# Hybrid encoder trunk on one core: where the second half of V's work sits at the turn from dots to dense products

## What is computed

```
def peer(xn, wq, k1, k2, u, v):
    ...                                     # idx: (token, 128) experts, gate: their softmax
    def block(args):                        # 128 tokens
        x_blk, i_blk, g_blk = args
        act = gelu(einsum('td,ted->te', x_blk, u[i_blk]))
        return einsum('te,ted->td', g_blk * act, v[i_blk])
    return lax.map(block, (xb, ib, gb))
```

## Time and profile before

| | |
|---|---|
| median of 3 runs | 3210.08 us (3208.91 to 3210.76) |
| the profiled execution: its time, its span | 3210.99 us, 3209.2 us |
| busy share of the span | DVE 77%, PE 68%, POOL 51%, ACT 27% |
| DMA over the span | 1096.32 MB, mean 342 GB/s |
| one gather of u: POOL's issue | 1.78 us, 496 of them |
| one dot on DVE | 2.29 us, 512 of them |
| one V addition on DVE | 1.28 us, 456 of them |
| TensorE's granted clock, mean | 0.841 of full speed |

### The profile page before, as it was taken

The page is one execution under the profiler, slowest core; times in us unless marked ns, Lnnn a source line. Parts: engine busy times, 40 slices in busy tenths (PEclk is TensorE's granted clock), DMA queues, the critical chain, the costliest instruction groups (busy, mean ns, idle before and its releaser), DMA issues.

```text
span 3209.2 us, 23725 instructions
## 1 busy us (share of the span) xinstructions
PE 2180.4 (68%) x7652; PEld 1394.4 (43%) x7652; DVE 2474.9 (77%) x3537; ACT 856.6 (27%) x1749; POOL 1621.2 (51%) x1051
## 2 busy tenths in 40 slices
PE   7999984440233348999979999444014344799999
PEld 6887773330121234444437878333012223444444
DVE  4454588999999986655575767999999998766666
ACT  4344410000555672000003442000036556400000
POOL 1000045666788834655560103555677884466665
PEclk9999996775567689999999999676556666999999
DMA  6554589999999957999994437999999997699999
GB/s 231 184 184 144 183 339 417 418 406 370 417 416 420 420 234 305 414 413 411 412 368 139 163 107 305 406 422 403 395 390 416 421 419 298 243 414 413 414 413 379
DMA packets 231210, 1096.32 MB, mean 342 GB/s; under 512 B 23208, under 2 KB 23984, under 8 KB 144176
## 3 DMA queue, kind: packets, MB, share of 16 engines
q0 software_dynamic: 147456, 805.37, 62.0%
q1 hardware_dynamic: 80256, 282.22, 23.2%
q10 hardware_dynamic: 3376, 7.23, 0.7%
HBM read 1092.63 MB, written 2.11 MB: 341 GB/s over the span
## 4 chain that ended last, share of the span: by engine, by line
DVE 32%; DMA 29%; PE 19%; issue 9%; POOL 8%; ACT 4%; ACTq 0%; DVEq 0%; SPq 0%; POOLq 0%
DVE ring_sb L1996 20%; PE bank L1118 15%; DMA actT_sb<-in_peer_vg_dram,idx_all 13%; DMA ring_sb<-in_peer_vg_dram,idx_all 8%; DMA ring_sb<-in_peer_u_dram,idx_all 6%; POOL ring_sb L639 5%; DVE x_sb L1970 3%; POOL actT_sb L656 2%; ACT ring_sb L904 1%; POOL ring_sb L656 1%; DVE shared L1709 1%; DVE shared L1705 1%; DVE pair_all L1713 1%; PE bank L1328 1%; POOL ring_sb L615 0%
## 5 line engine op out<-in xcount | busy, mean ns | idle before, releaser
L639 POOL DMA_INDIRECT ring_sb<-in_peer_u_dram,idx_all x496 | 880.8, 1776 | 378.1 <-DVE idx_all L1714 236.1
L1996 DVE CUSTOM_DVE_ANT_0 ring_sb<-ring_sb,actT_sb 128x2048 f32<-128x2048 f32 x256 | 572.5, 2285 | 26.1 <-DMA ring_sb<-in_peer_u_dram,idx_all 25.8
L1996 DVE CUSTOM_DVE_ANT_0 ring_sb<-ring_sb,arena 128x2048 f32<-128x2048 f32 x256 | 574.6, 2285 | 21.2 <-DMA ring_sb<-in_peer_u_dram,idx_all 19.6
L1970 DVE SCALAR_TENSOR_TENSOR x_sb<-actT_sb,gate_rows,x_sb 128x1024 f32<-128x1024 f32 x300 | 384.4, 1284 | 214.4 <-DMA actT_sb<-in_peer_vg_dram,idx_all 212.0
L1118 PE MATMUL bank<-w_parts,actT_hi 128*128 128x512 f32 x1664 | 521.0, 394 | 7.0 <-DVE w_parts L445 4.9
L656 POOL DMA_INDIRECT actT_sb<-in_peer_vg_dram,idx_all x300 | 370.3, 1234 | 296.0 <-DVE x_sb L1970 247.6
L1408 PE MATMUL bank<-ring_sb,arena 128*128 128x512 f32 x1024 | 481.3, 592 | 2.3 <-issue 2.3
L1408 PE MATMUL bank<-ring_sb 128*128 128x512 f32 x1024 | 481.2, 592 | 0.0
L1384 PE MATMUL bank<-gain 128*128 128x128 f32 x768 | 144.5, 351 | 411.8 <-ACT gain L885 386.5
L1165 PE MATMUL bank<-arena 128*128 128x256 f32 x896 | 248.1, 443 | 233.0 <-DVE shared L1996 233.0
L445 DVE TENSOR_TENSOR w_parts<-ring_sb,w_parts 128x2048 fp32r<-128x2048 f32 x100 | 229.3, 2298 | 211.9 <-ACT w_parts L439 211.8
(11 more groups left out here) (214 smaller groups left out, 2193.5 us busy)
## 6 DMA issues: line engine op xcount, KB each, us to landing
ring_sb<-in_peer_vd_dram SPq DMA_DIRECT2D x128, 1024.0 KB, 8.0
ring_sb<-in_mlstm_w_in_dram SPq DMA_DIRECT2D x48, 1024.0 KB, 5.1
arena<-in_peer_wq_dram SPq DMA_DIRECT2D x28, 1024.0 KB, 13.6
ring_sb<-in_attn_w_in_dram SPq DMA_DIRECT2D x20, 1024.0 KB, 5.1
ring_sb<-in_mlstm_w_out_dram SPq DMA_DIRECT2D x16, 1024.0 KB, 5.0
ring_sb<-in_attn_w_out_dram SPq DMA_DIRECT2D x16, 1024.0 KB, 5.0
ring_sb<-in_peer_u_dram,idx_all POOLq DMA_INDIRECT x496, 11.5
actT_sb<-in_peer_vg_dram,idx_all POOLq DMA_INDIRECT x300, 10.2
```

The costliest lines, as they stand in the source:

```text
L639: nc.gpsimd.indirect_dma_start(out=ring[i % NU], out_offset=None, in_=u_tab[l], in_offset=bass.IndirectOffsetOnAxis(ap=rows_at, axis=0),). ...
L1970: v.scalar_tensor_tensor(out=xb[b][:, DENSE:D], in0=g_slot[G_SLOT[j]], scalar=w_all[b][:, p:p + 1], in1=xb[b][:, DENSE:D], op0=ALU.mult, o ...
L1996: v.tensor_tensor_reduce(ring[i % NU], ring[i % NU], rows[b], 1.0, 0.0, ALU.mult, ALU.add, dots[u % 2][:, k:k + 1]).then_inc(dot_done, 1)
```

## The change

The first three loads of the ordered half all wait for the layer's last dot and for the last use of the rows gathered ahead. DVE makes no addition among the groups; all 228 come behind the last one. The gathers take the six places in plain order, so that gather 4 is the first in place 4, and the wait for all groups' products stands ahead of it.

```diff
@@ -334,8 +334,7 @@
         G_ALL = len(G_ORDER)
         G_LAST = [max(j for j in range(G_ALL) if G_ORDER[j][0] == b) for b in range(NB)]
         G_SAME = [max([-1] + [i for i in range(j) if G_ORDER[i][0] == G_ORDER[j][0]]) for j in range(G_ALL)]
-        G_EARLY = 12
-        G_SLOT = [j % 4 if j < G_EARLY else (j - G_EARLY) % NG for j in range(G_ALL)]
+        G_SLOT = [j % NG for j in range(G_ALL)]
         G_USE = [G_SLOT[:j].count(G_SLOT[j]) for j in range(G_ALL)]
         G_BEFORE = [max([-1] + [i for i in range(j) if G_SLOT[i] == G_SLOT[j]]) for j in range(G_ALL)]
 
@@ -526,11 +525,10 @@
             def load_dense(l):
 
                 for p in range(D_PAIRS):
-                    if p < ND - 1:
-                        sp.wait_ge(dot_done, l * LAYER_TILES + LAYER_TILES - NU + 2 + p + 1)
-                    elif p < ND:
+                    if p == 0:
+                        sp.wait_ge(dot_done, (l + 1) * LAYER_TILES)
                         sp.wait_ge(ahead_used, (l + 1) * N_AHEAD)
-                    else:
+                    if p >= ND:
                         sp.wait_ge(vd_used, l * D_PAIRS + p - ND + 1)
                     sp.dma_start(d_slot[p % ND], vd_tab[l][p]).then_inc(vd_landed[p % ND], 16)
                     if l == 0 and p in KEYS_BEHIND:
@@ -649,7 +647,7 @@
                     pool.wait_ge(idx_ready, (l + 1) * UNITS)
                 elif j < 4:
                     pool.wait_ge(ahead_used, (l + 1) * N_AHEAD)
-                if j == G_EARLY + 4:
+                if j == 4:
                     pool.wait_ge(wb_full, (2 * l + 2) * GROUPS)
                 if G_BEFORE[j] >= 0:
                     pool.wait_ge(vg_added, l * G_ALL + G_BEFORE[j] + 1)
@@ -2026,8 +2024,6 @@
                 wait_groups(dve, GR[f"t{l}"] + 1, 1)
                 for g in range(GROUPS):
                     weighted_group(g)
-                    if g % 4 == 3:
-                        add_value()
                 while added[0] < G_ALL:
                     if l == 0 and added[0] in KEYS_SPLIT:
                         lo_weights(dve, 16, [KEYS_SPLIT.index(added[0])])
```

## The result

The changed kernel takes 3217.2 us (median of 14 runs, 3213.43 to 3219.57), the kernel before 3211.16 beside it (3208.86 to 3214.86). The ratio is 1.0018 with a 95% interval of 1.0011 to 1.0026: some 6 us slower, where 4.4 were forecast. The profiled execution has a span of 3215.3 us against 3209.2. In a later series the same kernel had 1.0014 (1.0004 to 1.0023), 4.6 us. So the price is some 5 or 6 us by the medians, and the two intervals leave anything from 1 to 8.

A forecast was written before the change was run, and what follows sets the result against it. DMA bandwidth and PE's dense products bound the dense stage nearly alike. Layer 1: -7.4 + 0 + 10.2 - 0.5 = +2.3; layer 2: -7.1 + 0 + 9.7 - 0.5 = +2.1; gave 3214.5 us, range 3204 to 3224.

The forecast's parts named there:

- The three loads: At each layer's last dots: loads moved behind the last dot bring it and T0 7.4 and 7.1 us sooner.
- Additions among the groups cost nothing: In the second block's one-hot groups: taking eight additions out changes the time by 0, since ACT paces at 3.53 us per two groups.
- The rival of 9.6 us: In the one-hot groups: DVE sets the pace, so T0 comes a further 9.6 us sooner per layer; 3195.3, chance 0.04.
- Seven additions more at the end: At each layer's end: seven gathers and additions left for the dense stage add 10.2 us in layer 1, 9.7 in layer 2.
- 0.5 us regained at the start: At the dense stage's start: six free places let POOL issue six gathers in a row, gaining 0.5 us per layer.
- DVE paces: In the one-hot groups: DVE, not ACT, is the limit, T0 a further 9.6 us sooner per layer; 3195.3, chance 0.04.
- absorbed: In the dense stage: hidden slack takes up the seven gathers, leaving only the earlier T0; 3195.6, chance 0.05.
- the first part does nothing: At the last dots: the pace of U gathers, not the three loads, holds the last dot; 3229.0, chance 0.06.
- The restart held by late additions: At POOL's first issue after its wait: an unfinished addition holds it, shifting each layer 3.2 us; 3220.9, chance 0.13.
- The weighed rule: At POOL's issues beside additions: the skill's no-delay rule would cost 0.4 us less in all (3214.1); the measured row was preferred.

The follow-up runs named there:

- the first part alone: The kernel before with only its three first ordered loads made to wait for the last dot; 3195.33 us, ratio 0.9953.
- The third load alone: The kernel before with only the third ordered load moved behind the last dot, the first two at their old waits; 3207.98 us, ratio 0.999.
- ACT relieved: The changed kernel, but DVE builds three of four one-hot halves of the second block's groups, not every other one; 3204.81 us, ratio 0.9984.

## Why the prediction was right, point by point

- **The three loads, -7.4 and -7.1 us.** Measured -7.5 and -7.1 on the dots, and -14.7 for the first part alone against -14.5. The third load alone takes one of the three gaps away. Shown.
- **Additions among the groups cost nothing.** T0 lies 62 us behind the last dot with none, four or eight additions and with ten of them. Taking half of ACT's one-hot halves away shortens the groups by 6.6 to 8.1 us, and a quarter of them by 1.5 to 2.5, so ACT's pace is shown. The rival of 9.6 us falls.
- **Seven additions more at the end, 10.2 and 9.7 us, less 0.5 each.** Over the kernels in which ACT has its old share of work and the gain load its place (for layer 2 also those with the gain load of layer 1 late), layer 1 ends at 463.5 to 464.2 with 4 additions by T0 and layer 2 at 449.0 to 450.2; with 11 they end at 454.6 to 455.7 and 438.5 to 440.8. The means differ by 8.8 and 10.0 us, 18.8 for the two layers where 18.9 were forecast, and in the changed kernel the additions end 24 us behind PE in layer 1 and 10.5 in layer 2, where 25 and 8 were. With 7 additions both lie between: 461.5 and 444.9. So the price rises as the count falls, though not in even steps: in layer 1 the step from 11 to 7 costs 6.4 us on the mean and that from 7 to 4, where the order of places changes as well, only 2.3; in layer 2 they are 5.5 and 4.6. That the sum came out is in part luck, because the split between the layers was off, 0.9 us too much in layer 1 and 0.8 too little in layer 2, and the two errors cancel. In layer 1 the term "0.5 us regained at the start" was too small, by the gain load that the prediction didn't name: its 1 MB is 2.5 us of DMA time at 413 GB/s and went into the idle start. With it late, seven gathers cost 467.4 - 456.1 = 11.3 us there, by one trace each. In layer 2 nothing is regained: its first 15 us moved 321 GB/s, fewer than the 336 of the earlier trace rows, so that term had the wrong sign; over the like kernels it was 316 to 331 with four additions against 326 to 345 with eleven.
- **Where the 1.6 us beyond the forecast come from.** They are within the interval of the measurement, 3.5 to 8.4 us. The sum of these terms is 18.8 - 14.6 = 4.2 us. The profiled pair differs by 6.1, of which the parts that the change acts on are +0.6 us in layer 1 and +3.8 in layer 2 (+2.3 and +2.1 forecast); the rest is -1.1 us before the change acts and +2.7 between layer 1's end and the last dots of layer 2. From the last addition of layer 1 to the end of layer 2's last dot it took 1015.2 to 1018.3 us in the nine traces in which the three loads are late, 1017.7 of them in the changed kernel; in the three in which they are early it took 1022.2 to 1023.3, the least of them in the kernel before, and that is 1015.1 to 1016.2 without the 7.1 of the loads. So the kernel before was at the short end in its trace and the changed one towards the long end. Nothing in the change acts in this stretch; why it varies stays open.
- **The rivals.** "DVE paces", "absorbed" and "the first part does nothing" fell. The restart held by late additions didn't happen in the changed kernel, whose four additions end 0.7 us before POOL's wait, as forecast. It did where DVE was nearer to its limit: with ACT relieved, with one more half in eight on DVE and with an addition behind every third group, in both layers.
- **The weighed rule.** The Trainium skill (SBUF — State Buffer, "Who interferes with whom") states, and marks as inferred, that an operation of DVE with two SBUF inputs doesn't hold up GpSimd's writing of descriptors. Here the issue beside back-to-back additions took 4.13 us, and 3.53 and 2.21 in the kernel with ACT relieved, and ended 0.8 us behind the last of the additions; alone it took 0.94 us. For this issue the trace doesn't agree. The same section says that an operation with two SBUF inputs does contend with a GpSimd instruction that reads SBUF, and a gather reads its list idx_all from there; whether that is the reason no run here separates.

## What to carry to other kernels

When the DMA engines are the bound on both sides of a gap in which they idle, ask of every transfer on which side of the gap it lies: three loads moved from the full side into the gap gave back their whole time, and seven gathers moved out of the gap cost 8.8 and 10.0 us, 1.3 and 1.4 us each, where half a MB at 413 GB/s is 1.27. An engine's busy share doesn't say who paces a stage of four buffers (DVE had 54.95 of 55.70 us and still was not it); the constant period on one engine gave it away here, and taking work off that engine proved it. And where a queue restarts from a wait, see whether another engine's operations lengthen the issue (back-to-back additions did here), and keep them out of the microseconds in which it restarts.

## What was not expected of the hardware

- One indirect DMA's issue on POOL takes 0.94 us alone and up to 4.13 us when V additions run back to back on DVE. In the eight traces where such an issue meets the additions behind the groups, in both layers, it ended 0.8 us behind the last of them, whether it had begun 3.3, 2.7 or 1.4 us before their end. Beside one-hot operations it stayed at 0.94 us (1185.80 in the earlier trace rows).
- A transfer of 1 MB on a third queue at the moment of a restart took nothing from the others when the gathers had not yet filled the DMA engines (396 against 330 GB/s, the whole MB), and the layer ended 3.2 to 3.8 us sooner than with the transfer late. With eleven additions, where gathers are on their way at T0, 0.4 to 1.5 us of that were left.
